# First time-mix slots read input chunks written during the embedding pairs; both norm sums in a row; TensorE's layer loop written out twice

## The reference

```python
        gate = jax.nn.sigmoid(rms_norm(x, norm3_g[l]) @ w_pg[l])
        x = x + (p[l] @ w_pe[l]) * gate
    return rms_norm(x, final_g)
...
    for l in range(DEPTH_2):        # DEPTH_2 = 2
        x = hybrid_layer(x, norm1_g[l], w_in[l], ...)
...
    h = _rms(x) * norm1_g
    proj = h @ w_in
    aq, ak, av, rw, rq, rk, rv, rg, gates = _split(proj, IN_SIZES)
```

## Time and profile before

| | |
|---|---|
| median of 3 runs | 2651.93 us (2650.45 to 2653.21) |
| the profiled execution, its own time | 2652.36 us |
| its span in the trace | 2650.4 us |
| PE busy | 2595.0 us, 98% of the span |
| DVE, ACT, POOL busy | 1445.4, 644.4, 1488.3 us |
| mean granted clock of PE | 0.994 of full speed |

### The profile page before, as it was taken

One profiled execution on the slowest core, in us unless ns is written; L12 is line 12 of the kernel. 1 busy time (PEld: TensorE's weight loads), 2 busy tenths in 40 slices (PEclk: granted clock), 3 DMA queues, 4 the chain that ended last, 5 costly groups with the idle time before them and its releaser, 6 DMA issues.

```text
span 2650.4 us, 47417 instructions
## 1 busy us (share of the span) xinstructions
PE 2595.0 (98%) x16376; PEld 2025.7 (76%) x16376; DVE 1445.4 (55%) x2031; ACT 644.4 (24%) x1226; POOL 1488.3 (56%) x945
## 2 busy tenths in 40 slices
PE   8999999998999999999999999999999999999999
PEld 5778888876777677777888887777677777888887
DVE  6876555455467647764443434467647764443434
ACT  3452000024134423431200002134423431200002
POOL 4656666655544454556666666544454556666664
PEclk9999999999999999999999999999999999999999
DMA  4213233323221132223223333311132223333332
GB/s 153 76 37 113 93 95 95 95 75 112 87 57 37 48 93 64 72 74 101 91 92 94 95 95 111 93 57 38 47 93 64 72 75 100 93 90 94 95 95 95
DMA packets 72725, 222.67 MB, mean 84 GB/s; under 512 B 9344, under 2 KB 12544, under 8 KB 72576
## 3 DMA queue, kind: packets, MB, share of 16 engines
q1 hardware_dynamic: 72288, 220.60, 27.3%
q10 hardware_dynamic: 288, 0.04, 0.0%
HBM read 218.50 MB, written 2.10 MB: 83 GB/s over the span
## 4 chain that ended last, share of the span: by engine, by line
PE 92%; DVE 4%; DVEq 2%; issue 1%; POOL 1%; DMA 1%; ACT 0%; ACTq 0%; POOLq 0%; SPq 0%
PE acc L502 81%; PE bank L502 10%; PE bank L1102 0%; POOL w_lo L364 0%; DMA raw<-in_w_pg 0%; DVEq L1585 0%; DVE rw_bon L1140 0%; DVEq L1678 0%; DVE rw_SCB L1140 0%; DVE z_rw L1140 0%; DVE xg_lo L1234 0%; DVE y_lo L1140 0%; DVE y_hi L1147 0%; DVE z_rw L1623 0%; DVE z_rw L1625 0%
## 5 line engine op out<-in xcount | busy, mean ns | idle before, releaser
L364 POOL TENSOR_TENSOR w_lo<-raw,w_hi 128x1024 fp32r<-128x1024 f32 (+3 forms) x438 | 964.4, 2202 | 306.8 <-PE acc L502 279.1
L357 POOL TENSOR_SCALAR w_hi<-raw 128x1024 fp32r<-128x1024 f32 (+3 forms) x438 | 434.2, 991 | 668.1 <-PE acc L502 576.1
L502 PE MATMUL acc<-xg_hi,w_hi 128*128 128x512 f32 x2224 | 595.3, 405 | 15.6 <-issue 8.9
L502 PE MATMUL acc<-xg_hi,w_lo 128*128 128x512 f32 x2224 | 585.0, 399 | 0.0
L502 PE MATMUL acc<-xg_lo,w_hi 128*128 128x512 f32 x2224 | 584.8, 399 | 0.0
L502 PEld LDWEIGHTS acc<-xg_hi,w_hi 128*128 128x128 f32 x2224 | 413.5, 189 | 134.0 <-issue 40.1
L502 PEld LDWEIGHTS acc<-xg_lo,w_hi 128*128 128x128 f32 x2224 | 416.1, 188 | 103.5 <-issue 4.8
L502 PEld LDWEIGHTS acc<-xg_hi,w_lo 128*128 128x128 f32 x2224 | 414.8, 188 | 100.3 <-issue 0.5
L1957 ACT ACTIVATE ffn_act<-ffn_t 128x512 f32<-128x512 f32 x100 | 63.3, 633 | 773.5 <-DVEq L1200 619.5
L1140 DVE TENSOR_TENSOR x<-x,acc 128x512 f32<-128x512 f32 x104 | 71.4, 687 | 318.9 <-PE acc L502 318.4
L502 PE MATMUL acc<-hid_hi,w_hi 128*128 128x512 f32 x656 | 182.8, 396 | 3.7 <-POOL w_lo L364 1.6
(11 more groups left out here) (343 smaller groups left out, 2802.2 us busy)
## 6 DMA issues: line engine op xcount, KB each, us to landing
raw<-in_w_up SPq DMA_DIRECT2D x132, 512.0 KB, 3.6
raw<-in_w_down SPq DMA_DIRECT2D x48, 512.0 KB, 3.6
raw<-in_w_gate SPq DMA_DIRECT2D x48, 512.0 KB, 3.6
raw<-in_w_ret SPq DMA_DIRECT2D x32, 512.0 KB, 3.6
raw<-in_w_rw SPq DMA_DIRECT2D x28, 512.0 KB, 3.7
raw<-in_w_o SPq DMA_DIRECT2D x48, 256.0 KB, 2.7
raw<-in_w_in SPq DMA_DIRECT2D x18, 512.0 KB, 3.7
raw<-in_w_down SPq DMA_DIRECT2D x24, 384.0 KB, 3.0
```

The lines of the kernel that those rows point to most:

```text
L357: nc.gpsimd.tensor_scalar(w_hi[:, s, 0:n], raw[:, s, 0:n], 1.0, 0.0, ALU.mult, ALU.add).then_inc(w_half[s], 1)
L364: nc.gpsimd.tensor_tensor(w_lo[:, s, 0:n], raw[:, s, 0:n], bits(w_hi[:, s, 0:n]), ALU.subtract).then_inc(w_split[s], 1)
L502: return nc.tensor.matmul(o, a, b, start=first, stop=last, skip_group_check=shared)
```

## The change

Five things:

1. During the embedding pairs ACT writes, after `finished(j)`, a drain and one more activation: chunk j of layer 0's input into `hid_hi`. Only this raises `hi_ready`. DVE then does `squares(j-1)` and a new `copied(j-1)`, which writes the low part into `copy_lo`, and it does both **before** `embedding_gate(j)`.
2. PE's first two slots of layer 0 are written out in `first_pair`. They take chunks 0 to 6 from the copies and only chunk 7 from `xg`. They start with `acc_free[0]`, before the norm sum is there.
3. The two norm sums run one behind the other, over `sumsq_fin` into bank 4 and over `sumsq` into bank 5. The sum of the second norm is made by DVE from bank 4 in bank 5 itself, with no product of PE's.
4. ACT loads its table ahead of the last `finished`, and no longer in `roots`; chunk 7 goes ahead of the others; the low parts of chunks 4 to 6 come behind the second sum.
5. PE's loop over the layers is a Python loop: its code stands twice in the program.

```diff
+        copy_lo = [hid_lo[:, c, :] for c in range(DC - 2)] + [hid_hi[:, DC - 1, :]]
...
-            stats(4)
-
-            with pe.Fori(0, LAYERS) as l:
+
+            def first_pair(I):
+
+                def high(s, c, hi, lo):
+                    w = w_hi[:, s, c * P:(c + 1) * P]
+                    mm(acc[s][:], w, hi, c == 0, False)
+                    return mm(acc[s][:], w, lo, False, False)
+
+                def low(s, c, hi):
+                    return mm(acc[s][:], w_lo[:, s, c * P:(c + 1) * P], hi, False, c == DC - 1)
+
+                pe.wait_ge(w_half[0], I + 1)
+                pe.wait_ge(acc_free[0], I + 1)
+                for c in range(DC - 1):
+                    pe.wait_ge(copy_ready, c + 1)
+                    high(0, c, hid_hi[:, c, :], copy_lo[c])
+                pe.wait_ge(w_split[0], I + 2)
+                for c in range(DC - 1):
+                    low(0, c, hid_hi[:, c, :])
+                pe.wait_ge(w_half[1], I + 1)
+                pe.wait_ge(acc_free[1], I + 1)
+                high(1, 0, hid_hi[:, 0, :], copy_lo[0])
+                pe.wait_ge(sumsq_ready, 4)
+                mm(bank[4][:], K["ones"][:], sumsq_fin, True, True)
+                mm(bank[5][:], K["ones"][:], sumsq[:], True, True).then_inc(stat_ready, 1)
+                c = DC - 1
+                pe.wait_ge(xg_ready, 3 * DC + 2)
+                high(0, c, xg_hi[:, c, :], xg_lo[:, c, :]).then_inc(hi_done[0], 1)
+                low(0, c, xg_hi[:, c, :]).then_inc(slot_done[0], 1)
+                for k in range(1, DC - 1):
+                    high(1, k, hid_hi[:, k, :], copy_lo[k])
+                high(1, c, xg_hi[:, c, :], xg_lo[:, c, :]).then_inc(hi_done[1], 1)
+                pe.wait_ge(w_split[1], I + 2)
+                for k in range(DC - 1):
+                    low(1, k, hid_hi[:, k, :])
+                low(1, c, xg_hi[:, c, :]).then_inc(slot_done[1], 1)
+                pe.wait_ge(xg_ready, 4 * DC)
+
+            for l in range(LAYERS):
...
-                late(0, I, xg, full, xg_ready, DC * (2 * l + 3))
-                stats(2 * l + 5)
-                slot(1, I, xg, full)
+                if l == 0:
+                    first_pair(I)
+                else:
+                    late(0, I, xg, full, xg_ready, DC * (2 * l + 3))
+                    stats(2 * l + 5)
+                    slot(1, I, xg, full)
...
+            def copied(c):
+                v.scalar_tensor_tensor(copy_lo[c], x[:, c, :], K["gains"][:, G_L, c:c + 1], bits(hid_hi[:, c, :]),
+                                       ALU.mult, ALU.subtract).then_inc(copy_ready, 1)
+
             for j in range(PE_PAIRS):
-                embedding_gate(j)
                 if j > 0:
                     squares(j - 1, j)
+                    copied(j - 1)
+                embedding_gate(j)
                 embedding(j)
...
-            tt(sumsq[:], sumsq_fin, rstd[:])
-            dve.drain()
-            tt(sumsq[:], sumsq[:], rstd[:])
-            dve.drain()
+            tt(bank[5][:], bank[4][:], rstd[:])
+            dve.drain()
+            tt(bank[5][:], bank[5][:], rstd[:])
+            dve.drain()
+            dve.sem_inc(stat_ready, 1)
             dve.sem_inc(sumsq_ready, 1)
+            for c in range(4, DC - 1):
+                low_half(c, DC + 2 + c)
...
                 if j < PE_PAIRS - 1:
                     finished(j)
-            act.drain()
+                    act.drain()
+                    fn(hid_hi[:, j, :], x[:, j, :], ACT.Identity, scale=K["gains"][:, G_L, j:j + 1]).then_inc(hi_ready, 1)
+            table(LOG_EXP)
             act.wait_ge(slot_done[0], B1_PAIRS + 1)
             for c in range(2):
                 high_half(c)
-            finished(DC - 1)
-            for c in range(2, DC - 1):
-                high_half(c)
+            finished(DC - 1).then_inc(hi_ready, 1)
             act.drain()
             high_half(DC - 1)
-            roots(4)
+            for c in range(2, 4):
+                high_half(c)
+            roots(4, False)
+            for c in range(4, DC - 1):
+                high_half(c)
 
             with act.Fori(0, LAYERS) as l:
-                roots(2 * l + 5)
+                roots(2 * l + 5, False)
```

More of the change, by code:

```diff
@@ L240, in build @@
         sumsq_ready, stat_ready, root_ready = sem("sumsq_ready"), sem("stat_ready"), sem("root_ready")
+        copy_ready = sem("copy_ready")
         square_in, zero_in = sem("square_in"), sem("zero_in")
@@ L1534, in low_half @@
                                        ALU.mult, ALU.subtract).then_inc(xg_ready, 1)
+            def copied(c):
+                v.scalar_tensor_tensor(copy_lo[c], x[:, c, :], K["gains"][:, G_L, c:c + 1], bits(hid_hi[:, c, :]),
+                                       ALU.mult, ALU.subtract).then_inc(copy_ready, 1)
             for j in range(PE_PAIRS):
-                embedding_gate(j)
                 if j > 0:
                     squares(j - 1, j)
+                    copied(j - 1)
+                embedding_gate(j)
                 embedding(j)
-            for c in range(2):
-                low_half(c, DC + c)
+            low_half(0, DC)
             squares(DC - 1, DC + 2)
@@ L1545, in _ @@
             dve.sem_inc(sumsq_ready, 1)
-            for c in range(2, DC):
-                low_half(c, DC + 1 + c)
+            low_half(DC - 1, DC + 3)
+            low_half(1, DC + 1)
+            for c in range(2, 4):
+                low_half(c, DC + 2 + c)
             dve.wait_ge(root_ready, 4)
             v.tensor_copy(rstd_fin, rstd[:])
-            tt(sumsq[:], sumsq_fin, rstd[:])
+            tt(bank[5][:], bank[4][:], rstd[:])
             dve.drain()
-            tt(sumsq[:], sumsq[:], rstd[:])
+            tt(bank[5][:], bank[5][:], rstd[:])
             dve.drain()
+            dve.sem_inc(stat_ready, 1)
             dve.sem_inc(sumsq_ready, 1)
+            for c in range(4, DC - 1):
+                low_half(c, DC + 2 + c)
             vec2 = K["vec2"]
@@ L2156, in finished @@
                 fn(bank[4 - 4 * (j % 2)][:], x[:, j, :], ACT.Square, scale=K["gains"][:, G_FIN, j:j + 1])
-                fn(x[:, j, :], x[:, j, :], ACT.Identity, scale=K["gains"][:, G_FIN, j:j + 1]).then_inc(hi_ready, 1)
+                return fn(x[:, j, :], x[:, j, :], ACT.Identity, scale=K["gains"][:, G_FIN, j:j + 1])
             def high_half(c):
```

## The result

| | before | changed |
|---|---|---|
| median | 2652.36 us (18 runs) | 2656.82 us (18 runs) |
| lowest to highest | 2649.94 to 2654.58 | 2652.03 to 2666.18 |
| ratio | | 1.0018, interval 1.0012 to 1.0024 |
| profiled execution | 2652.36 us | 2660.64 us |

The changed kernel is slower by 0.18%, 4.5 us, just inside the 0.2% that the prediction called indistinguishable from no change, but its interval doesn't reach 1. Its runs are spread more than twice as wide as those of before. The profiled execution is one of the long ones, 3.8 us over the median, so its trace shows more loss than the usual run has.

The account below looks back on a forecast made before the run. PE, busy 98%, was taken to bound the kernel. From 2652.4, +0.7 (later next pair), +2.5 (low clock) and -1.06 (turn) gave 2654.5, less 0.4 to the median: 2654 us, range 2644.5 to 2662.

Parts of the forecast that it names:

- likeliest case: Whole kernel: PE's stall and low clock move one pair later; 2654 us, own range 2650 to 2658, chance 0.4.
- Ring in the pairs: Embedding pairs: DVE and ACT form a serial ring of 7.55 us from gate to gate, against a mean of 7.35.
- I take 7.8: Embedding pairs: POOL's round taken as 7.8 us, 0.45 over the mean; seven rounds cost 3.2 us.
- The lock: DVE instructions with two SBUF inputs and POOL's lock each other out; POOL pays 0.5 us if DVE is first.
- End of the pairs: Before layer 0: slot matmuls fill the 6.26 us hole, PE waits 1.1 us for sums, both slots done at 665.6.
- Where the stall goes: Slot 0 of the next pair: starts at 671.9, 0.7 us later, behind a new 6.3 us hole; low clock costs 2.5.
- The turn: Layer 0 to layer 1: writing out PE's loop removes a hole of 1.06 us.
- The bursts: Small-matmul bursts in the layers: writing out could change holes by -3.4 to +3.4 us; taken as 0.
- the rival on code loading: Bursts of small matmuls: the four holes double, +3.4 us on top, 2657.5 us; chance 0.05.
- The sum of the steps: Whole kernel: 2652.4 + 0.7 + 2.5 - 1.06 = 2654.5, less 0.4 to the median: 2654 us.
- POOL gets in first: Embedding pairs: `w_lo` begins before `copied`, 2.2 us for each pair, one to seven: 2656 to 2669 us; chance 0.2.
- The gain is real: Next pair: low parts and `rstd` miss POOL, slot 0 at about 668: 2647.7, or 2642 to 2645 us; chance 0.25.

Follow-up runs that it names:

- Experiment 2: Kernel before with only the embedding-pair edits (ACT's extra activation, DVE's squares and low copy ahead of the gate), copies unread: 2657.17 us, ratio 1.0019.
- experiment 3: Changed kernel with DVE's gate first in each embedding pair, then squares and low copy of the chunk before: 2654.74 us, ratio 1.0013.
- Experiments 4: Changed kernel with low parts of chunks 1 to 6 copied from the low copies, all ahead of the norm's root: 2653.46 us, ratio 1.0003.
- experiment 5: Changed kernel with gate first in the pairs and low parts copied ahead of the root: 2650.96 us, 0.9995; with DVE's constants also moved earlier: 2652.11 us, 0.9998.
- experiment 6: Unread matmuls filling a hole: 20 behind slot 1 in the changed kernel, 2653.39 us, 1.0004; 25 ahead of the norm sum in the kernel before, 2650.81 us, 0.9990.

## Why the prediction came out as it did

The direction of the likeliest case, a stall moved and not removed, was right, and 2654.0 lies 2.8 us under the 2656.82 measured. That it lies so near is in part luck, as the steps show: two terms were too high, one was taken at nothing and was not nothing, and 1.3 us of the profile have to do with no term. Step by step, with times as they stand in the profile:

- **Ring in the pairs.** Right in its mechanism and length: 7.55 us from gate to gate was computed, and the pairs take 7.52 to 7.62. DVE gets in ahead of POOL's `w_lo`, the case taken. The step "I take 7.8" was wrong, for it priced POOL's ring with 3.95 us from the freed `raw` to `w_hi` and a delay of 0.5; in the changed program the first is 3.6 to 3.8, since the load itself takes 3.2 in place of 3.6, and `w_lo` pays 0.2. The first product was forecast for 652.4 and came at 652.92, but only because of the 1.3 us that were there ahead of the pairs: by themselves the pairs cost 2.6 us and not 3.3. The cost of the pairs was named only as a shift of that start. Experiment 2 measures the edits of the pairs at 1.0019, with the longer loads of the loop in it, and in experiment 3 the order of DVE's instructions alone brings the pairs back to 7.0 to 7.2.
- **The lock.** The Trainium skill, SBUF — State Buffer, section "Who interferes with whom", also says that DVE's copies and `tensor_scalar` in a mode with two ports take the same lock. The traces agree: the copy of `rstd` took 0.43 us in the changed kernel and 2.62 with gate first beside a `w_lo`, and the constant of 14 columns took 2.31. I had put the constants at "0.1 to 0.2", which held in the changed kernel (0.17 and 0.28) only by luck.
- **End of the pairs.** Wait for the sums 0.80 us (forecast 1.1), sums at 659.33 (659.0), both slots done at 667.15 (665.6). The sums and the 25 matmuls behind them take 7.8 us where 6.7 were forecast, at full clock. With the 1.3 us of the start taken off, the sums come 1.0 earlier than forecast.
- **Where the stall goes.** Slot 0 of the next pair at 672.43 (671.9), hole 5.28 us (6.3), three low parts 1.8 us each ("0.8 to 1.9"). Less the 1.3 us of the start, slot 0 comes when it came before: the "0.7 later" did not happen. Experiments 4 and 5 show it by taking the low parts away. The clock falls behind the hole: 2.2 us (2.5), shown by experiment 6.
- **The turn.** Gone; 1.1 us (1.06).
- **The bursts.** "I take 0" is the step that failed in size. In the profiled execution the bursts of layer 0 are 5.4 us longer, by three holes of 1.2 to 1.6 us and a lowered clock behind the last. In the other seven profiles with the layers written out they are from 1.2 shorter to 2.1 longer, in the five with the loop besides that of before from 0.2 shorter to 0.3 longer. So writing out does make them uneven, as far as 14 profiles show, for which the rival on code loading had a chance of 0.05. The Trainium skill's rule on fetching (Runtime: NRT & Kernel Launch, section "Instruction fetch mechanics"), that straight code is fetched ahead, does not cover these holes: they stand in straight code. Whether fetching makes them is not shown.
- **The sum of the steps.** Without the bursts the profile gives +1.3 (next pair) + 2.2 (clock) - 1.1 (turn), 2.4 us, against the 2.1 forecast (0.7 + 2.5 - 1.06). That is luck: the 1.3 us were there before any edited instruction, and what the steps themselves give is 1.1. The median is 4.5 over before, so some 3.4 us are left, and what makes them and the long runs up to 2666 is settled only in part. The bursts of layer 0 are the one place where the profile shows more, 5.4 us, in one long execution. Runs with the lower mean granted clock are the long ones (0.996 at 2653.2, 0.995 at 2655.1, 0.994 at 2657.8, 0.993 at 2661.9, medians); filling the new hole narrows nine of eleven runs to 2652.4 to 2653.8, with two at 2656.5 and 2658.6; and keeping the loop narrows them too, though its one long run, 2665.18, has a mean clock of 0.995. Holes with a lowered clock behind them are the likely sum, but which hole it is in a long run without a profile stays open.

Of the rivals, "POOL gets in first" happened with `w_lo` in no pair; the shorter `w_hi` was ahead of the copy, for 0.5 us at the most. "The gain is real" needed low parts that meet nothing; experiment 5 made that case by hand and came to 2650.96, where the rival's sum said 2647.7. In its profile slot 0 of the next pair is 4.0 us earlier than before and the turn gives 1.1, and the bursts of layer 0 take 1.5 back, those of layer 1 0.5. Its interval (0.9986 to 1.0004) does not show it to be faster than before.

## What to carry to other kernels

Work pulled forward into an idle stretch of one engine is only won if the next thing that engine waits for comes earlier too: follow the instruction that frees its next buffer, and keep everything else behind it. Put the instruction on which the bottleneck waits first in its engine's order, and the work done ahead for later behind it: here that order alone made a pair of 7.0 to 7.2 us one of 7.5 to 7.6. Keep DVE instructions that can meet POOL off that path. A one-input copy in place of a computation with two inputs in SBUF is shorter (0.4 us against 0.8 where neither meets POOL), but it is no protection: beside `w_lo` such a copy took 2.65 us, and a constant of 14 columns 2.31. And before two traces are subtracted, look how far apart they are already ahead of the edit.

## What the runs showed of the hardware

- A program with PE's layers written out has its 512 KB weight loads in 3.2 us, the same with the loop in 3.5 to 3.7, on the same chip. Nothing in the transfers was changed. Why is open; where the program and its tensors lie in memory may differ, which was not tried. That holds for one profiled execution of each of the 14 kernels.
- PE's clock falls behind some holes of 2.3 us and holds behind others of the same length and place: the second pair took 8.6 us in 10 of the 13 profiles without matmuls in that hole, and 7.06 in three. One such row, with the loop:

```profile
598.48:607.10 8.62, 8.62 (x30) 6.84 (x31) 2.45 (x4) 3.61 (x6) 2.25 (x3) 0.80 0.25 78
```

- Matmuls whose result nobody reads, in a hole of 6.3 us, made a kernel 0.1% faster (0.9990, 0.9981 to 0.9999).
- A DVE instruction on 128x14 elements took 2.31 us, and a copy with one input 2.65 in place of 0.42, each beside a `w_lo` of 2.34 to 2.40 us that POOL had begun 0.06 and 0.03 us before.
